# Routing between the output projection and the experts, rebuilt: all groups' choices at once, prefix counts by doubling sums, tile numbers by rounding, the one-hot in four parts

## The chip, the cores and the metric

One Trainium2 chip, one of its cores. The metric is the device time of one execution in microseconds; the executions of the kernel before are compared by their median. All data are float32.

## The reference, cut to what matters

One trunk layer on 256 context and 1,024 latent tokens (T = 1,280, D = 1,024): mixers, then a mixture of experts, then a last norm. The change touches only the choice of experts and the lists made from it:

```
gp = softmax(t @ w_rg + b_rg)              # 4 groups
g_top, g_idx = top_k(gp, 1)
el = (t @ w_re + b_re).reshape(T, 4, 4)    # 4 experts in each group
ep = softmax(el of the chosen group)
e_top, e_idx = top_k(ep, 2)
wts = e_top / sum(e_top) * g_top
y = sum over the two experts of wts * (silu(t @ w_gate) * (t @ w_up)) @ w_down
```

## The kernel before

Five instruction streams (PE, DVE, ACT, POOL, SP) are written out by hand, each in the order of the source, and meet on counting semaphores. Nothing is scheduled by a program. Every VectorE (DVE) operation of the routing waits for the one ahead of it (`dve_chain`); the ones that another engine waits for count `dve_once` up, and TensorE (PE) answers on `pe_once`.

Tokens stand in NT = 10 tiles of 128. After the output projection, each tile gets its normed rows `h2`, which SP stores to HBM (`h2_store`), while `x2_store` stores the residual. `router` (PE, L1278) multiplies the turned rows by the routers' 20 columns, and `logits` (DVE, L2089) puts them into `lg`: per tile 4 columns of groups and 4 x 4 of experts. Then the routing runs once for all tokens:

1. DVE chooses the group (`top`, five operations on 10 x 4), picks out its four logits with a one-hot (`r_big`, L2192), chooses the first and the second expert (`top` twice), and makes `m_one`, `m_two` and their sum `m_all`: 16 columns for each of 10 tiles, and an empty eleventh (L2203 to L2207). ACT computes the exponentials for the weights meanwhile (L1628), which DVE turns into `wts` (L2217 to L2225).
2. PE counts, for each token and expert, the tokens ahead of it: a product with a triangle (L1300) for those of its own tile, and ten products with ones (L1302), 160 to 16 columns wide, for those of earlier tiles.
3. DVE turns counts into the number of slot tiles of each expert (L2231 to L2250) and a slot for each of the 2 x 10 choices of a token (`r_pos`, L2256). A slot number is split in a tile (one of MT = 35, `r_hi`) and a lane (one of 128, `r_lo`): 36 thresholds are compared and summed (L2259, L2261), their differences are the one-hot `r_hot` (L2265). From it come `r_hot_w` (times the weight) and `r_hot` (times the token's number), and `r_lane` is the lane's one-hot, 20 x 128 (L2271).
4. PE adds up 20 products of `r_lane` with `r_hot` (L1307), which give the token of every slot, and 20 with `r_hot_w` (L1310), which give its weight. Meanwhile DVE makes the tables `tab_i` of expert addresses (L2275 to L2287), then, from the first product, the list `slot_i` (L2290).
5. POOL gathers the rows of a slot tile from HBM by `slot_i` (L2510), PE turns them (`turn_slots`, L1320), ACT copies them (L1636), and `gate_up` (L1325), `hidden` and `down` (L1335) follow, for 35 slot tiles. SP loads experts' weights into a ring of four: experts 0 to 2 during the routing, expert 3 only when the routing's scratch, over which it lies, is free. `landing_told` passes the arrival of an expert's weights on to PE.

Of the kernel before, what the change touches and what calls it, by code (L numbers as in the profile page):

```python
# [18 lines left out]
ALU = mybir.AluOpType  # L19
# [3 lines left out]
P = 128  # L23
# [4 lines left out]
NT = T // P  # L28
# [12 lines left out]
RING_E = len(RING_AT)  # L41
COL = dict(aq=0, ak=512, av=640, dq=768, dk=1280, dv=1792, ba=2304, dgate=2336, gattn=2848, gdn=3872)
# [32 lines left out]
def small_constants():  # L75
# [3 lines left out]
            [float(at[e + 1] - at[e]) if e + 1 < NE else 0.0 for e in range(NE)], 128.0 * np.arange(MT + 1), np.arange(P) - 128.0, [4, 3, 2, 1],  # L79
# [15 lines left out]
def build(nc, a, outs):  # L95
    ctx = ExitStack()
    with ctx:
# [47 lines left out]
        slot_step, k128, lane, first4, turn_of = small_row(NE), small_row(MT + 1), small_row(P), small_row(4), small_row(NE)  # L145
# [351 lines left out]
        r_gm, r_m1, r_m2, r_seen = [rsc(NT, 1) for _ in range(4)]  # L497
        r_ohg, r_oh1, r_oh2, r_key, r_el, r_el2 = [rsc(NT, 4) for _ in range(6)]
        r_e5 = rsc(NT, 5)
        r_big = rsc(NT * NE)  # L500
        m_both = rsc(2, NT * NE)
        m_all = rsc(NT + 1, NE)
# [4 lines left out]
        r_hi, r_lo, tok_f = rsc(2 * NT), rsc(2 * NT), rsc(2 * NT)  # L507
        r_ge, r_hot = rsc(2 * NT, MT + 1), rsc(2 * NT, MT)
        r_tab = rsc(HT + MT + NE)
        r_hot_w = flat(r_ge)[:, 0:2 * NT * MT].rearrange("p (j t) -> p j t", t=MT)  # L510
# [20 lines left out]
        def _(sp):  # L531
# [273 lines left out]
        def _(pe):  # L805
# [492 lines left out]
            router(OUT_LAST)  # L1298
            pe.wait_ge(S["dve_once"], 7)
            mm(ps[:, 4, 0:(NT + 1) * NE], before, flat(m_all), start=True, stop=False)  # L1300
            for n in range(NT):
                last = mm(ps[:, 4, (n + 1) * NE:(NT + 1) * NE].rearrange("p (n e) -> p n e", e=NE), ones,  # L1302
                          m_all[:, n, :].unsqueeze(1).to_broadcast([P, NT - n, NE]), start=False, stop=(n == NT - 1))
            last.then_inc(S["pe_once"], 1)
            pe.wait_ge(S["dve_once"], 8)
            for j in range(2 * NT):
                last = mm(ps[:, 5, 0:MT], r_lane[:, j, :], r_hot[:, j, :], start=(j == 0), stop=(j == 2 * NT - 1))  # L1307
# [352 lines left out]
        def _(dve):  # L1660
# [507 lines left out]
            for t in OUT_PAIRS[-1] + (OUT_LAST,):  # L2168
                logits(t)
# [378 lines left out]
```

## Time and profile before

| | |
|---|---|
| Median of 3 executions | 2233.24 us (2230.2 to 2241.52) |
| Profiled execution: its own time | 2229.11 us |
| Its span in the trace | 2227.2 us |
| Busy share: PE, DVE, ACT, POOL | 91%, 48%, 29%, 17% |
| Granted TensorE clock, mean | 0.954 |

The times below are microseconds from the span's start. PE's records come in pairs: one float32 product is two records, so 20 products are "x40". In the lists of busy time a stage in which an engine waits hardly shows; it is read from the order of time.

### The profile page before, as it was taken

To read this page: it belongs to the slowest core of one execution; us is meant where nothing else is said; L and a number is where in the kernel's file an instruction comes from. 1 tells how busy PE (TensorE), PEld (TensorE's weight loads), DVE (VectorE), ACT (ScalarE), POOL (GpSimd) and SP (SyncE) were. 2 spreads that over 40 slices of the span, in tenths; PEclk is the share of its full clock that TensorE was granted. 3 is DMA by queue.
4 is the path that set the end of the run, shared out by engine and by line. 5 is a ranking of instruction groups with operands and counts; after the bars stand their busy time and mean duration, and the time that the engine had idled before them with its cause. 6 is when DMAs were issued, how large, how long until landed. Compare 5 with 4: busy or idle time off the path is not lost.

```text
span 2227.2 us, 40085 instructions
## 1 busy us (share of the span) xinstructions
PE 2022.2 (91%) x16735; PEld 1291.7 (58%) x16735; DVE 1063.1 (48%) x1868; ACT 640.2 (29%) x1329; POOL 381.6 (17%) x431
## 2 busy tenths in 40 slices
PE   4998999999999868888799999999899699999992
PEld 3556567676455457777656666666445644444441
DVE  2256665663687556656464223222554423333334
ACT  5222666663445323442330100100111111111112
POOL 2000100000000135543103122111220012222210
PEclk8999999999999979999999999999999599999996
DMA  9523300001010044443303232232333767698646
GB/s 335 170 76 116 84 5 2 1 1 58 21 32 0 13 64 76 77 74 63 102 0 104 62 81 57 58 84 76 136 111 123 238 190 201 185 282 231 185 76 217
DMA packets 261329, 226.44 MB, mean 102 GB/s; under 512 B 106588, under 2 KB 223648, under 8 KB 260256
## 3 DMA queue, kind: packets, MB, share of 16 engines
q1 hardware_dynamic: 249856, 184.98, 29.0%
q0 software_dynamic: 11296, 38.91, 7.8%
q8 instruction: 135, 2.21, 0.4%
q14 instruction: 42, 0.34, 0.0%
HBM read 175.15 MB, written 48.55 MB: 100 GB/s over the span
## 4 chain that ended last, share of the span: by engine, by line
PE 46%; DVE 3%; DMA 1%; ACT 1%; issue 0%; SPq 0%; DVEq 0%; ACTq 0%; POOLq 0%; PEldq 0%
PE ps L1176 17%; PE ps L1325 11%; PE ps L1335 5%; PE ps L1223 4%; PE ps L1164 3%; PE ps L1320 1%; PE ps L1278 1%; PE ps L1217 1%; DVE R L2350 1%; PE ps L1154 0%; PE ps L1268 0%; DMA R<-in_w_out_dram 0%; DMA R<-attn_out_scratch 0%; PE ps L1307 0%; PE ps L1310 0%
## 5 line engine op out<-in xcount | busy, mean ns | idle before, releaser
L1176 PE MATMUL ps<-R 128*128 128x320 f32 x1280 | 353.2, 436 | 3.0 <-DVEq L2040 2.3
L1176 PEld LDWEIGHTS ps<-R 128*128 128x128 f32 x1280 | 243.3, 191 | 110.7 <-DVE R L2079 7.9
L899 PE MATMUL ps<-R 128*128 128x512 f32 (+1 forms) x816 | 298.9, 525 | 4.9 <-DVE R L1707 1.8
L1325 PE MATMUL ps<-R 128*128 x560 | 248.8, 598 | 3.2 <-ACT R L1636 2.3
L899 PEld LDWEIGHTS ps<-R 128*128 128x128 f32 x816 | 155.4, 192 | 143.4 <-issue 132.2
L1325 PEld LDWEIGHTS ps<-R 128*128 128x128 f32 x560 | 107.4, 192 | 138.2 <-issue 138.2
L1773 DVE TENSOR_SCALAR_CACHE_REDUCE R<-ps 128x512 f32<-128x512 f32 (+1 forms) x208 | 128.3, 666 | 56.7 <-PE ps L995 56.6
L1335 PE MATMUL ps<-R 128*128 x280 | 126.2, 594 | 1.6 <-DVE R L2333 1.6
L1014 PEld LDWEIGHTS ps<-cst,R 128*128 128x128 f32 x800 | 86.4, 142 | 57.6 <-issue 45.9
L2333 DVE COPY R<-ps 128x256 f32<-128x256 f32 x35 | 14.8, 424 | 216.4 <-PE ps L1350 216.4
L1487 ACT ACTIVATE R<-R 128x1536 f32<-128x1536 f32 (+1 forms) x80 | 108.6, 1358 | 12.5 <-DVE R L1782 12.4
L1014 PE MATMUL ps<-cst,R 128*128 128x128 f32 x800 | 105.1, 280 | 4.5 <-ACT R L1497 2.9
L995 PE MATMUL ps<-R 64*128 64x512 f32 (+1 forms) x416 | 106.6, 616 | 2.3 <-SPq L590 2.1
L1645 ACT ACTIVATE R<-ps 128x256 f32<-128x256 f32 x35 | 13.4, 384 | 323.0 <-PE ps L1325 323.0
L2397 POOL TENSOR_TENSOR R<-cst,R 128x512 f32<-128x512 f32 x20 | 20.4, 1040 | 491.0 <-DVE R L1805 491.0
L1067 PE MATMUL ps<-R 64*64 64x64 f32 x2464 | 86.7, 226 | 15.7 <-issue 9.9
L1028 PE MATMUL ps<-R 128*64 128x128 f32 x1600 | 96.5, 276 | 0.5 <-ACT R L1513 0.5
L1497 ACT ACTIVATE R<-ps 128x512 f32<-128x512 f32 (+1 forms) x144 | 75.4, 571 | 73.6 <-PE ps L1014 73.2
L1223 PE MATMUL ps<-R 128*128 128x512 f32 x200 | 92.9, 619 | 2.4 <-DVE R L2098 2.4
L1067 PEld LDWEIGHTS ps<-R 64*64 64x64 f32 x2464 | 81.4, 141 | 18.6 <-issue 15.2
L1028 PEld LDWEIGHTS ps<-R 128*64 128x64 f32 x1600 | 86.8, 137 | 7.4 <-ACT R L1497 5.7
L2510 POOL DMA_INDIRECT R<-h_scratch,slot_i x35 | 34.3, 981 | 281.4 <-PE ps L1320 179.4
(343 smaller groups left out, 2885.6 us busy)
## 6 DMA issues: line engine op xcount, KB each, us to landing
R<-in_w_mod_dram SPq DMA_DIRECT2D x12, 2048.0 KB, 9.0
R<-in_w_in_dram SPq DMA_DIRECT2D x46, 512.0 KB, 5.4
R<-in_w_gate_e_dram SPq DMA_DIRECT2D x16, 1024.0 KB, 7.5
R<-in_w_up_e_dram SPq DMA_DIRECT2D x16, 1024.0 KB, 11.0
R<-in_w_down_e_dram SPq DMA_DIRECT2D x16, 1024.0 KB, 8.0
R<-tu_scratch SPq DMA_DIRECT2D x40, 256.0 KB, 4.4
R<-in_x_sample_dram SPq DMA_DIRECT2D x16, 512.0 KB, 6.7
token_sums<-R SPq DMA_DIRECT2D x10, 512.0 KB, 5.6
```

Source lines behind the costliest of these rows:

```text
L899: last = mm(ps[:, u % 4, 0:w], w_sb[n % NW][:, k, :], hT[:, k, c0:c0 + w], start=(k == 0), stop=(k == KD - 1))
L995: last = mm(ps[:, 2 * (u % 2) + g, 0:w], qT[lo, h4, qt * P:(qt + 1) * P], kT[lo, c0 + j * 512:c0 + j * 512 + w], start=True, stop=True)
L1014: last = turn128(ps[:, 4 + v % 3, k * P:(k + 1) * P], s_sb[i % 2][g][:, j * 512 + k * P:j * 512 + (k + 1) * P], ident)
L1028: last = mm(ps[lo, 7, (i % 4) * P:(i % 4 + 1) * P], v_sb[:, v0 + j, lo], pT[i % 2][g][:, j, :], start=(j == 0), stop=(j == nk - 1))
L1067: last = mm(ps[lo, bank, a * C:(a + 1) * C], lhs(a)[lo], rhs(a)[lo], start=True, stop=True)
L1176: last = mm(ps[:, bank, 0:HALF], lhs[:, k, :], rhs[:, k, :], start=(k == 0), stop=(k == 3))
L1223: last = mm(ps[:, bank, :], lhs[:, k, :], rhs[k], start=(k == 0), stop=(k == 3))
L1325: last = mm(ps[:, 2 + t % 2, :], hsT[t % 2][:, k, :], R[:, bass.ds(at + (RB + k * 512), 512)], start=(k == 0), stop=(k == KD - 1))
L1335: last = mm(ps[:, 5 + u % 3, :], hidT[t % 2][:, k, :], R[:, bass.ds(at + (RB + 4096 + k * D + h * 512), 512)], start=(k == 0), stop=(k == 1))
L1487: f(s_sb[i % 2][g][:, 0:w], s_sb[i % 2][g][:, 0:w], ACT.Exp, bias=shift[i % 2][g], accum_out=sums[qt % 2][:, g, h4:h4 + 1]).then_inc(S["p_ ...
L1497: f(pT[i % 2][g][:, 4 * j:4 * j + w // P, :].rearrange("p n c -> p (n c)"), ps[:, 4 + v % 3, 0:w], ACT.Copy).then_inc(S["pt_act"], 1)
L1773: v.tensor_scalar(s_sb[i % 2][g][:, j * 512:j * 512 + w], ps[:, 2 * (u % 2) + g, 0:w], HD ** -0.5, None, ALU.mult, ALU.max, accum_out=tops ...
```

## The change

- The choices of all four groups are made along with that of the group: `top` works on the 50 rows of 4 in `lg` (5 for each tile), twice instead of three times, and the chosen group masks the result. `m_all` is made first and lies in a zeroed strip `m_led`.
- The sums over earlier tiles are made by DVE (`r_sum2`, `r_sum4`, `r_sum8`, each the one before added to itself moved by 1, 2, 4 tiles, and then 8), and PE needs one product with ones in place of ten. PE's product with the triangle starts as soon as `m_all` is there.
- The tile of a slot is its number times 1/128, rounded by adding 1.5 x 2^23; `r_hot` is one comparison with 35 constants. `r_tok` is a tile of its own.
- `r_lane` is made in four parts of 2, 6, 6 and 6 choices, and PE starts on each as it comes.
- The weights (`r_e5`, ACT's exponentials, `wts`, `r_hot_w`) are made behind the one-hot; the last of them stand behind the tables and ahead of `slot_i`. `r_hot_w` lies in the residual's tile, so it waits until SP's stores of it have landed (`sp_out`).
- Of the 20 products that give the weights of the slots, 10 stand ahead of the first `turn_slots`, 10 ahead of the second `gate_up`; their result is copied in the second round.
- SP tells of the landing of experts 0 and 1 first, and loads expert 3 after the first two gathers have landed.
- The zeroing of `m_led` and three small operations stand ahead of the last logits.

The diff, with the repeated waits on `dve_chain` and the tile names' bookkeeping left out:

```diff
+ROUND = 1.5 * 2 ** 23
...
+        m_led = R3[:, 8960:8960 + (3 * NT + 11) * NE].rearrange("p (n e) -> p n e", e=NE)
+        m_pad, r_sum2, r_sum4 = m_led[:, 0:NT + 3], m_led[:, NT + 3:2 * NT + 6], m_led[:, 2 * NT + 6:]
+        m_all, r_sum8 = m_pad[:, 2:NT + 3, :], rsc(NT + 1, NE)
...
+        r_tok = R3[:, 8192:8192 + 2 * NT * MT].rearrange("p (j t) -> p j t", t=MT)
+        r_hot_w = R0[:, 0:2 * NT * MT].rearrange("p (j t) -> p j t", t=MT)
+        LANE_PARTS = ((0, 2), (2, 8), (8, 14), (14, 20))
...
             expert_load(2)
-            sp.wait_ge(S["dve_once"], 9)
-            sp.wait_ge(S["pe_once"], 5)
+            landing_told(0)
+            landing_told(1)
+            sp.wait_ge(S["dve_once"], 13)
             for n in (NT - 2, NT - 1):
                 sp.wait_ge(S[f"h2_out{n % 2}"], landed(n, 2))
+            for t in range(2):
+                sp.wait_ge(S[f"hs_in{t}"], 16)
             expert_load(3)
-            landing_told(0)
-            landing_told(1)
...
+            pe.wait_ge(S["dve_once"], 6)
+            mm(ps[:, 4, 0:(NT + 1) * NE], before, flat(m_all), start=True, stop=False)
             pe.wait_ge(S["dve_once"], 7)
...
+            mm(ps[:, 4, 0:(NT + 1) * NE], ones, flat(r_sum8), start=False, stop=True).then_inc(S["pe_once"], 1)
+            for part, (first, end) in enumerate(LANE_PARTS):
+                pe.wait_ge(S["dve_once"], 8 + part)
+                for j in range(first, end):
+                    last = mm(ps[:, 5, 0:MT], r_lane[:, j, :], r_tok[:, j, :], start=(j == 0), stop=(j == 2 * NT - 1))
             last.then_inc(S["pe_once"], 1)
...
+            def slot_weights(first, end):
+                for j in range(first, end):
+                    last = mm(ps[:, 7, 0:MT], r_lane[:, j, :], r_hot_w[:, j, :], start=(j == 0), stop=(j == 2 * NT - 1))
+                return last
+
+            pe.wait_ge(S["dve_once"], 13)
+            slot_weights(0, NT)
...
+                    if t == 1:
+                        slot_weights(NT, 2 * NT).then_inc(S["pe_once"], 1)
...
-            act.wait_ge(S["dve_once"], 6)
+            act.wait_ge(S["dve_once"], 12)
...
+            top(lgs, r_m1, r_oh1)
+            v.scalar_tensor_tensor(r_el2, r_oh1, -3e38, lgs, ALU.mult, ALU.add).then_inc(S["dve_chain"], 1)
...
             top(r_el2, r_m2, r_oh2)
...
+            v.tensor_tensor(r_key, r_oh1, r_oh2, ALU.add).then_inc(S["dve_chain"], 1)
...
+            v.tensor_tensor(by_group(m_all[:, 0:NT, :]), by_row(r_key)[:, :, 1:5, :], in_group, ALU.mult).then_inc(S["dve_once"], 1)
...
+            v.tensor_tensor(r_sum8[:, 8:NT + 1, :], r_sum8[:, 8:NT + 1, :], r_sum8[:, 0:NT - 7, :], ALU.add).then_inc(S["dve_once"], 1)
...
+            v.tensor_scalar(r_hm, pos, 1.0 / SLOTS, ROUND, ALU.mult, ALU.add).then_inc(S["dve_chain"], 1)
...
+            for first, end in LANE_PARTS:
+                v.tensor_tensor(r_lane[:, first:end, :], bc(r_lo[:, first:end].unsqueeze(2), [end - first, P]), bc(lane.unsqueeze(1), [end - first, P]), ALU.is_equal).then_inc(S["dve_once"], 1)
+                dve.wait_ge(S["dve_once"], count("dve_once"))
...
+            dve.wait_ge(S["sp_out"], 288 + 16 * NT)
+            v.tensor_tensor(r_hot_w, r_hot, bc(flat(wts).unsqueeze(2), [2 * NT, MT]), ALU.mult).then_inc(S["dve_chain"], 1)
...
             dve.wait_ge(S["pe_once"], 4)
             v.tensor_scalar(slot_i[:], ps[:, 5, 0:MT], -1.0, 0.0, ALU.add, ALU.max).then_inc(S["dve_once"], 1)
```

Line numbers of the kernel after are 8 to 27 higher. The order of DVE's instructions from the slots' numbers to the one-hot of the lanes, before (thresholds, their sum, lane, differences, weights, tokens, lanes, first table) and after (rounding, one-hot, tokens, tile, lane, lanes in two rows, weights' exponents, first table):

```order
L2259 TENSOR_TENSOR R<-R,small 128x720
L2261 TENSOR_REDUCE R<-R 128x20
L2263 SCALAR_TENSOR_TENSOR R<-R 128x20
L2265 TENSOR_TENSOR R<-R 128x700
L2267 TENSOR_TENSOR R<-R,wts 128x700
L2269 TENSOR_TENSOR R<-R 128x700
L2271 TENSOR_TENSOR R<-R,small 128x2560
L2275 TENSOR_TENSOR R<-small,R 128x560
```

```order
L2264 TENSOR_SCALAR R<-R 128x20
L2266 TENSOR_TENSOR R<-R,small 128x700
L2268 TENSOR_TENSOR R<-R 128x700
L2270 TENSOR_SCALAR R<-R 128x20
L2272 SCALAR_TENSOR_TENSOR R<-R 128x20
L2275 TENSOR_TENSOR R<-R,small 128x256
L2275 TENSOR_TENSOR R<-R,small 128x768 x3
L2278 TENSOR_TENSOR R<-R 128x10x4
L2280 TENSOR_TENSOR R<-R 128x50
L2282 TENSOR_TENSOR R<-R 128x40
L2284 TENSOR_REDUCE R<-R 128x10
L2288 TENSOR_TENSOR R<-small,R 128x560
```

Two operations as long as the tables' are gone, the long one is four, and four small ones stand between it and the tables. The order of DVE's instructions from the tables' end to `slot_i`, which before are L2285 to L2290 and after L2298 to L2317:

```order
L2283 TENSOR_REDUCE R<-R 128x35
L2285 TENSOR_SCALAR R<-R 128x16
L2287 CAST tab_i<-R 128x86
L2290 TENSOR_SCALAR slot_i<-ps 128x35
L2302 TENSOR_SCALAR mod_row<-ps 128x35
```

```order
L2298 TENSOR_SCALAR R<-R 128x16
L2300 CAST tab_i<-R 128x86
L2303 TENSOR_REDUCE R<-R 128x10
L2305 TENSOR_SCALAR R<-R 128x10
L2307 TENSOR_TENSOR R<-R 128x10
L2309 RECIPROCAL wts<-R 128x10
L2311 TENSOR_TENSOR wts<-wts,R 128x10
L2314 TENSOR_TENSOR R<-R,wts 128x700
L2317 TENSOR_SCALAR slot_i<-ps 128x35
```

Six operations of the weights have moved in ahead of `slot_i`. The order of PE's products from the end of the counting to the first turn of gathered rows, before and after (one row is a product here, not two records):

```order
L1302 MATMUL ps<-R,cst 128x32
L1302 MATMUL ps<-R,cst 128x16
L1307 MATMUL ps<-R 128x35 x20
L1310 MATMUL ps<-R 128x35 x20
L1320 MATMUL ps<-cst,R 128x128 x8
```

```order
L1308 MATMUL ps<-R,cst 128x176
L1310 MATMUL ps<-R,cst 128x176
L1314 MATMUL ps<-R 128x35 x20
L1319 MATMUL ps<-R 128x35 x10
L1331 MATMUL ps<-cst,R 128x128 x8
```

Ten of the weights' products have gone from the place ahead of the first turn; they stand behind the second turn now.

## Rows read from the trace of the kernel before

**Rows 1.** The chain that ended last, 1690 to 1830: start us, us, what
```profile
1762.80 8.75 PE ps L1307 x40
1771.55 8.55 PE ps L1310 x40
...
1781.19 1.14 SPq L755
...
1782.81 9.67 PE ps L1325 x16
...
1795.60 7.13 PE ps L1325 x16
...
1802.94 0.87 PE ps L1320 x8
```
**Rows 2.** Windows: us, PE, PEld, DVE, ACT, POOL busy (instructions), PEclk, DMA share, GB/s
```profile
1730.00:1760.00 30.00, 12.41 (x54) 11.67 (x54) 18.42 (x57) 2.72 (x4) 0.00 (x0) 0.50 1.06 362
...
1760.00:1765.00 5.00, 2.20 (x11) 2.20 (x11) 4.86 (x5) 0.00 (x0) 0.00 (x0) 0.50 0.40 156
...
1785.00:1790.00 5.00, 5.00 (x9) 1.98 (x9) 0.00 (x0) 0.00 (x0) 0.00 (x0) 0.71 1.05 365
```
**Rows 3.** Timeline of DVE, choices and weights: start us, busy us, line, op, tiles, shapes
```profile
1739.18 0.20 DVE L2172 TENSOR_REDUCE R<-R 128x10 f32<-128x40 f32 x1
1739.41 0.20 DVE L2174 TENSOR_TENSOR R<-R 128x40 f32<-128x40 f32 x1
...
1740.58 0.43 DVE L2192 TENSOR_TENSOR R<-R 128x160 f32<-128x160 f32 x1
...
1744.17 0.69 DVE L2203 TENSOR_TENSOR R<-R 128x160 f32<-128x160 f32 x2
...
1746.00 0.19 DVE L2217 TENSOR_REDUCE R<-R 128x10 f32<-128x40 f32 x1
...
1746.89 0.18 DVE L2225 TENSOR_TENSOR wts<-wts,R 128x10 f32<-128x10 f32 x1
```
**Rows 4.** Timeline of DVE, from the counts to the list of slots
```profile
1750.71 0.33 DVE L2231 TENSOR_TENSOR R<-ps,small 128x160 f32<-128x160 f32 x1 [3.64 <-PE ps L1302]
...
1755.05 0.91 DVE L2259 TENSOR_TENSOR R<-R,small 128x720 f32<-128x720 f32 x1
1756.00 0.90 DVE L2261 TENSOR_REDUCE R<-R 128x20 f32<-128x720 f32 x1
...
1762.78 0.74 DVE L2275 TENSOR_TENSOR R<-small,R 128x560 f32<-128x560 f32 x1
...
1766.30 0.21 DVE L2287 CAST tab_i<-R 128x86 int32<-128x86 f32 x1
1771.66 0.20 DVE L2290 TENSOR_SCALAR slot_i<-ps 128x35 uint32<-128x35 f32 x1 [5.15 <-PE ps L1307]
```
**Rows 5.** Timeline of PE around the routing
```profile
1705.77 3.65 PE L1278 MATMUL ps<-R 128*128 128x20 f32 x32
...
1735.26 3.60 PE L1278 MATMUL ps<-R 128*128 128x20 f32 x16 [0.73 <-ACT R L1605]
1745.41 0.95 PE L1300 MATMUL ps<-R,cst 128*128 128x176 f32 x2 [6.55 <-DVE R L2207]
...
1779.89 1.95 PE L1320 MATMUL ps<-cst,R 128*128 128x128 f32 x8
```
**Rows 6.** Timeline of POOL, the first gather's issue
```profile
1772.14 1.07 POOL L2510 DMA_INDIRECT R<-h_scratch,slot_i  x1 [101.68 <-DVE slot_i L2290]
```
**Rows 7.** DMA issues: first gather; residual's last store (issued 1734.67): us to landing
```profile
R<-h_scratch,slot_i POOLq DMA_INDIRECT x1, 4.4
...
token_sums<-R SPq DMA_DIRECT2D x1, 512.0 KB, 9.9
```
**Rows 8.** All 35 gathers, line L2510
```profile
DMA to landing us min/median/max: 4.2/4.8/8.5
```
**Rows 9.** Timeline of ACT, the table for the exponentials
```profile
1744.21 1.28 ACT L1628 ACT_TABLE_LOAD   x1 [9.00 <-DVE R L2200]
```

More of the change, by code:

```diff
@@ L78, in small_constants @@
     rows = [np.arange(T // SLOTS) * float(SLOTS), np.arange(HT), (np.arange(NE)[None, :] < np.arange(NE)[:, None]).ravel(),
-            [float(at[e + 1] - at[e]) if e + 1 < NE else 0.0 for e in range(NE)], 128.0 * np.arange(MT + 1), np.arange(P) - 128.0, [4, 3, 2, 1],
+            [float(at[e + 1] - at[e]) if e + 1 < NE else 0.0 for e in range(NE)], ROUND + np.arange(MT), np.arange(P) - 63.5, [4, 3, 2, 1],
             [int(f"{e:04b}"[::-1], 2) for e in range(NE)]]
@@ L1298, in _ @@
             router(OUT_LAST)
+            pe.wait_ge(S["dve_once"], 6)
+            mm(ps[:, 4, 0:(NT + 1) * NE], before, flat(m_all), start=True, stop=False)
             pe.wait_ge(S["dve_once"], 7)
[L1300 to L1303, printed above, removed]
-            last.then_inc(S["pe_once"], 1)
-            pe.wait_ge(S["dve_once"], 8)
-            for j in range(2 * NT):
-                last = mm(ps[:, 5, 0:MT], r_lane[:, j, :], r_hot[:, j, :], start=(j == 0), stop=(j == 2 * NT - 1))
-            last.then_inc(S["pe_once"], 1)
-            for j in range(2 * NT):
-                last = mm(ps[:, 4, 256:256 + MT], r_lane[:, j, :], r_hot_w[:, j, :], start=(j == 0), stop=(j == 2 * NT - 1))
-            last.then_inc(S["pe_once"], 1)
-            pe.wait_ge(S["dve_once"], 9)
+            mm(ps[:, 4, 0:(NT + 1) * NE], ones, flat(r_sum8), start=False, stop=True).then_inc(S["pe_once"], 1)
[3 more added lines that the diff above has]
+                    last = mm(ps[:, 5, 0:MT], r_lane[:, j, :], r_tok[:, j, :], start=(j == 0), stop=(j == 2 * NT - 1))
+            last.then_inc(S["pe_once"], 1)
+            def slot_weights(first, end):
[4 more added lines that the diff above has]
+            slot_weights(0, NT)
             def turn_slots(t):
@@ L2226, in _ @@
             dve.wait_ge(S["dve_chain"], count("dve_chain"))
+            v.tensor_tensor(r_sum8[:, 8:NT + 1, :], r_sum8[:, 8:NT + 1, :], r_sum8[:, 0:NT - 7, :], ALU.add).then_inc(S["dve_once"], 1)
+            dve.wait_ge(S["dve_once"], count("dve_once"))
+            for i, oh in enumerate((r_oh1, r_oh2)):
+                v.tensor_tensor(by_group(m_both[:, i, :].rearrange("p (n e) -> p n e", n=NT)), by_row(oh)[:, :, 1:5, :], in_group, ALU.mult).then_inc(S["dve_chain"], 1)
+                dve.wait_ge(S["dve_chain"], count("dve_chain"))
@@ L2272, in _ @@
+            v.tensor_reduce(r_e5[:, :, 4:5], r_gap, AX.X, ALU.add).then_inc(S["dve_once"], 1)
             dve.wait_ge(S["dve_once"], count("dve_once"))
```

126 lines of the change are left out of this document (62 added, 64 removed).

## The prediction

> **What bounds the kernel now.** I read the chain of work that ended last first. Among the experts it is TensorE (PE) alone, one slot tile behind the other, and nothing of that is changed. Ahead of it stands one long passage in which PE is mostly without work or at small work, and that is the change's place: from the first routing operation at 1739.18 [rows 3] to the first `gate_up` at 1782.81 [rows 1], 43.6 us. Whatever moves that start moves the end by as much, unless the first slot tiles give it back.
>
> The passage has five pieces, and the reader should see who is waited for in each. (a) 1739.18 to 1745.41: VectorE (DVE) chooses, and PE's count starts at 1745.41 [rows 3, 5]. (b) To 1750.71: DVE needs PE's counts, and its row says that it sat 3.64 us for L1302 [rows 4]. (c) To 1762.80: DVE alone, up to the one-hot of the lanes [rows 1, 4]. (d) 1762.80 to 1780.10 (1771.55 + 8.55): 40 products of 35 columns, 8.75 and 8.55 us [rows 1]. The first half ends at 1771.55 and `slot_i` follows at 1771.66 [rows 1, 4]; the gather is issued at 1772.14 and has landed 4.4 us later, at 1776.5 [rows 6, 7]. So the second half, 1771.55 to 1780.10, covers the gather and 3.6 us more. (e) Turns from 1779.89, and `gate_up` at 1782.81, released by SP's L755, the issue of expert 3's weights, which stands ahead of `landing_told(0)` [rows 1, 5].
>
> From 1730 on all of it runs at the granted clock 0.50, 1.2 GHz, and the clock comes back to 1.00 inside 1785 to 1790: the share 0.71 says 2.9 us of five at half, thus at about 1787.9, 5.1 us after `gate_up` began [rows 2].
>
> **A price for DVE.** From one start to the next an operation on 40 elements takes 0.23 us (1739.18 to 1739.41) and one on 720 takes 0.95 (1755.05 to 1756.00) [rows 3, 4]. The line through both is 0.19 us + 1.06 ns for each element: 160 cost 0.36, 176 0.37, 200 0.40, 256 0.46, 700 0.93, 768 1.00. Two rows bound it: two operations of 160 took 0.69 together, one with a stride 0.43 [rows 3]. The changed code reads with strides in a few places, so about 0.1 each is open.
>
> **The change, part by part.**
> *Choices.* Ahead of `m_all` stand 12 operations on 200 and one on 160: 4.80 + 0.36 = 5.16 us, so PE can begin at 1744.4 in place of 1745.41. The group's own choice is no longer a step of its own, but each step is five times as wide: a gain of only 1.0.
> *Prefix sums.* Three additions on 176 and one on 48: 3 x 0.37 + 0.24 = 1.36, done at 1745.7. The triangle's product (0.95 for a product of 176 [rows 5]) is behind them by then. The ones' product takes 0.95 more, to 1746.7, and DVE starts at 1746.8 where it started at 1750.71: 3.9 gained so far. The two masks for `m_both`, 0.7 us, lie beside PE's product.
> *To the one-hot.* The code up to `r_pos` is unchanged: 1750.71 to 1755.05, 4.34 us [rows 4], now ending at 1751.15. Then two of 700 and three of 20 elements: 1.86 + 0.63 = 2.49, to 1753.65, and the first part, 256 elements, to 1754.1. PE starts at 1754.15, not 1762.80: 8.65 gained. In place of seven operations stand six shorter ones, and PE no longer waits for the whole one-hot.
> *The products.* 40 records take 8.75, so one product takes 0.44. Two are done at 1755.0, the second part is there at 1755.1, each later part takes DVE 1.00 and PE 2.6, so PE runs on: 1755.15 + 18 x 0.44 = 1763.05. DVE could start on `slot_i` at 1763.15.
> *DVE's list ahead of `slot_i`.* Parts to 1757.1; four small operations, 0.94, to 1758.05; tables 1762.78 to 1766.54 before [rows 4], 3.76, to 1761.8; five for the weights, 1746.00 to 1747.10 [rows 3], 1.10; `r_hot_w` 0.93. Sum 1763.85: this, 0.7 later than PE's result, is what `slot_i` waits for. ACT has from 1758.05 to 1761.8 for a table load of 1.28 [rows 9] and the exponentials; hidden, by 2 us.
> *Gather.* Issued 0.48 behind the start of `slot_i`, 1764.3; landed 4.4 later, 1768.7. PE's ten products for weights run from 1764.1 to 1768.5: the cover and the gather end within 0.2 us, the gather last. Turns start at 1768.8 instead of 1779.89: 11.1 gained. With the cover cut in half it no longer costs anything, and the gather is what is late now.
> *To `gate_up`.* From the turns' start to `gate_up` it was 2.9 us. The wait for SP's issue is gone, since the landings are told first, but the turns end 1.95 after their start [rows 5] and ACT's last copy must still follow, so at most 1.0 can fall away, and likely little. I take 2.9 again: start at 1771.7, **11.1 us earlier**.
> *The other ten weights' products.* From the end of the first `gate_up` (1782.81 + 9.67 = 1792.48) to the second it is 3.12 us, in which PE turns (0.87) and then sits for ACT's sigmoid, with its table load, and copies [rows 1]. The ten products go there: 20 records at the full clock by 32 records in 3.65 us, 0.114 each [rows 5], are 2.28, and 0.87 + 2.28 = 3.15. They cost nothing within 0.1 as long as the clock is full; at half, by 16 records in 3.60 [rows 5], they are 4.5 and cost 2.2.
> *What else moves, at nothing.* Zeroing 656 elements (under 0.95, by the operation on 720 [rows 4]) and three small operations stand ahead of the last logits. These wait for PE's last router, 1735.26 to 1738.86 [rows 5], just ahead of the first choice at 1739.18; the zeroing lies beside it or before. Without that cover it costs 1.5. Expert 3 is loaded after two gathers, about 1771, not 1781, and its first tile is far off. The copy of the weights' result is 0.2 on DVE, which has spare time beside PE in each slot tile.
>
> *A rule against the row.* The first gather landed 4.4 us after issue [rows 7]. The Trainium skill, page "DMA: Bandwidth & Descriptors", section "Anatomy of one DMA", gives for a transfer issued from GpSimd 2.0 us and its bytes over 436 GB/s; for 512 KB that is 3.2. By that figure, an estimate from the page, the products for weights would end last, and the gain would be 11.3. The sum above keeps to the row.
>
> **Sum.** 1.0 from the choices, 2.9 from the counts, 4.75 from the shorter way to the one-hot and its parts, minus 0.8 because `slot_i` now waits for DVE and not for PE's product, plus 3.3 since half the weights' products have left the passage (the gather's landing decides now). 11.15, less what rounding takes: **11.1**. The profiled execution took 2229.11 (span 2227.2), so it would be 2218.0; the median of the three is 2233.24, 4.1 above that execution, and from it I get **2222**. That is 0.50%, exactly the bound of about 0.5% that a measurement of this kernel can tell from no change. The sign is fairly sure and the class isn't.
>
> **The rivals.**
> *The clock comes back at another moment.* `gate_up` took 9.67 with 5.1 us at half, 7.13 at full [rows 1, 2]: 2.5 us were lost. If it comes back almost at once, gain up to 13.6, time 2219.6; if the whole first `gate_up` stays at half (14.3), and the ten products with it, gain 11.1 - 4.6 - 2.2 = 4.3, 2229; a half step of that, 8.5, 2225. For earlier: nothing but the spread. For later: the passage before it is shorter and has two more pauses. Earlier 15%, later 11%.
> *The gather is slow.* It is issued nearly 8 us earlier, closer to the loads of experts 0 to 2. The slowest of 35 took 8.5 us [rows 8]. Then gain 11.1 - 4.1 = 7.0, 2226. Against: traffic ended at about 1762 (a share of 0.40 in 1760 to 1765 [rows 2]), 2 us before the issue. 8%.
> *Cutting the one-hot costs a pause.* If a cut of a long DVE operation brought a pause about as long as a part, 1.0, instead of the 0.19 that the line gives, three cuts move the tables and `slot_i` by 2.4: gain 8.7, 2224.5. Against: the operation of 720 took 0.91 and the next began 0.04 later [rows 4]. 2%. The Trainium skill, page "VectorE: DVE Perf Modes", section "The DRAIN you can't avoid", has such a pause, the operation's duration less 266 ns, behind each operation; the trace doesn't agree.
> *Slower: `slot_i` is held by the residual's store.* `r_hot_w` waits for all stores of the residual, and `slot_i` stands behind it. The last store took 9.9 us among 9 MB of weights and landed at 1744.6 [rows 7]; DVE asks at 1762.9. Each us beyond costs one: at 1774.0 nothing is gained, and past 1785 it is slower by over 0.5%; a landing at 1790 gives 2249. Against: 18 us of room. 4%, with whatever else is on that side.
>
> **How the numbers follow.** The forecast (gain 9.5 to 12.8, thus 2220.4 to 2223.7) has 60%; a share of 35 lies above 0.5%, 25 below, as the centre is on the bound. Faster: 35 + 15 (early clock) = 0.50. Same: 25 + 11 + 8 + 2 = 0.46. Slower: 0.04. The range goes from the early clock less what three executions scatter (2219.6 - 3 = 2216) to a late clock or a slow gather with it (2226 + 4 = 2230). If the strided operations cost 0.1 more each and DVE's line is off by 5%, that is 1 us, inside it.
>
> **What would show it.** In the trace after: PE's counting product within 0.3 of 1744.4; DVE's first use of the counts at 1746.8; the first slot product at 1754.1 and the last ending by 1763.1; `slot_i` idle for nothing, right behind L2314, at 1763.85; the turns released by the gather; `gate_up` at 1771.7; 3.1 us from the end of the first to the second. Wrong if PE waits between the parts, if the turns start later than 1770, or if the second `gate_up` comes over 4 us behind the first.

## The result, and the profile after

Over eight timed runs of each kernel the changed one took 2219.36 us (2215.72 to 2223.43) and the one before 2231.76 (2230.2 to 2241.52): 12.4 us less. The ratio over all runs is 0.9941, with a 95% interval of 0.9926 to 0.9955: the changed kernel is faster by 0.45 to 0.74%. That is clear of no change, takes in the bound of 0.5% that the prediction named, and by a line of 2% would count as the same. The forecast was 2222 and a gain of 11.1. The profiled execution took 2222.26, its span 2220.4.

That span is only 6.8 us shorter than before's, and this is no contradiction. The first routing choice came at 1739.18 [rows 3] before and comes at 1745.38 now. In the executions of the changed kernel's repeat and of its variants below it came between 1737.3 and 1748.9, though all of them are the same up to the last router's product. So all times below are taken from the first choice, a row that each kernel has (`DVE L2172` before, the first `DVE L2193` now), up to the first `gate_up`. This stretch is called the passage.

Timeline of PE in the changed kernel (start us, busy us, line, operation, tiles, and in brackets the idle time ahead with what ended it), the answer to [rows 1, 5]:
```profile
1750.56 0.95 PE L1308 MATMUL ps<-R,cst 128*128 128x176 f32 x2 [5.50 <-DVE R L2219]
1751.93 0.96 PE L1310 MATMUL ps<-R,cst 128*128 128x176 f32 x2 [0.42 <-DVE R L2227]
1760.30 8.89 PE L1314 MATMUL ps<-R 128*128 128x35 f32 x40 [7.42 <-DVE R L2275]
1770.46 4.48 PE L1319 MATMUL ps<-R 128*128 128x35 f32 x20 [1.27 <-DVE slot_i L2317]
1775.03 1.97 PE L1331 MATMUL ps<-cst,R 128*128 128x128 f32 x8
1777.94 8.94 PE L1336 MATMUL ps<-R 128*128 x16 [0.94 <-ACT R L1649]
1786.72 1.04 PE L1331 MATMUL ps<-cst,R 128*128 128x128 f32 x8
1787.59 2.32 PE L1319 MATMUL ps<-R 128*128 128x35 f32 x20
1789.90 7.13 PE L1336 MATMUL ps<-R 128*128 x16
```
Timeline of DVE, the answer to [rows 3, 4]:
```profile
1745.17 0.18 DVE L2102 TENSOR_TENSOR R<-ps,b_r 128x20 f32<-128x20 f32 x1 [4.63 <-PE ps L1286]
1745.38 0.36 DVE L2193 TENSOR_REDUCE R<-R 128x50 f32<-128x200 f32 x1
...
1752.99 0.33 DVE L2236 TENSOR_TENSOR R<-ps,small 128x160 f32<-128x160 f32 x1 [0.40 <-PE ps L1310]
...
1759.82 3.40 DVE L2275 TENSOR_TENSOR R<-R,small 128x256 f32<-128x256 f32 x4
...
1769.28 0.89 DVE L2314 TENSOR_TENSOR R<-R,wts 128x700 f32<-128x700 f32 x1 [0.26 <-DVE wts L2311]
1770.21 0.19 DVE L2317 TENSOR_SCALAR slot_i<-ps 128x35 uint32<-128x35 f32 x1
```
The chain that ended last, where it leaves DVE:
```profile
1769.28 0.90 DVE R L2314
1770.68 4.30 DMA R<-h_scratch,slot_i
1775.03 1.98 PE ps L1331 x8
1777.10 0.61 ACT R L1649
1777.94 8.94 PE ps L1336 x16
```
And the windows (us, busy of PE, PEld, DVE, ACT, POOL, then the granted clock, DMA share, GB/s), the answer to [rows 2]:
```profile
1744.00:1759.00 15.00, 2.97 (x9) 1.95 (x9) 12.27 (x36) 0.00 (x0) 0.00 (x0) 0.50 1.06 381
1759.00:1776.00 17.00, 14.34 (x65) 14.00 (x66) 11.20 (x29) 1.53 (x2) 2.02 (x2) 0.50 0.77 260
1776.00:1781.00 5.00, 4.06 (x9) 2.11 (x8) 0.00 (x0) 1.19 (x2) 0.93 (x1) 0.50 0.45 144
1781.00:1786.00 5.00, 5.00 (x12) 2.09 (x11) 0.00 (x0) 0.00 (x0) 0.00 (x0) 0.94 0.99 356
```
DVE's first row shows that the zeroing and the small operations that now stand ahead of the last logits cost nothing, as the prediction had it: DVE still waits 4.63 for PE's last router there. DVE's wait for the counts is 0.40 where it was 3.64. PE begins the slot products with the first of four parts (`x4` in one row). The chain no longer has the second forty products in it: it goes from DVE over the gather to the turns.

In us behind the first choice:

| | before | predicted | after |
|---|---|---|---|
| PE's triangle product | 6.23 | 5.2 | 5.18 |
| DVE's first use of the counts | 11.53 | 7.6 | 7.61 |
| first slot product | 23.62 | 15.0 | 14.92 |
| `slot_i` | 32.48 | 24.67 | 24.83 |
| first gather landed | 37.3 | 29.5 | 29.6 |
| first turn | 40.71 | 29.6 | 29.65 |
| first `gate_up` | 43.63 | 32.5 | 32.56 |
| first `gate_up`, duration | 9.67 | 9.67 | 8.94 |
| its end to the second | 3.12 | 3.15 | 3.02 |

The passage is 11.07 shorter. From the first choice to the end it is 488.06 before and 475.02 after, 13.0 less: 11.07 of the passage, 0.72 of the first `gate_up`, 0.1 of the gap behind it, and 1.15 from the second `gate_up` to the end. At most 11.9 of that, up to the second `gate_up`, can be the change's. From the second to the 35th `gate_up` it takes 376.15 to 376.17 in all 14 profiled executions of this document, and from the 35th to the end 55.49 before, 54.33 after and 53.99 to 55.71 over the changed kernel and its variants: the 1.15 lies in that last stretch and within its scatter.

### The profile page after: what moved, and what is told of

It is laid out like the page before. It is cut to its first block, busy times and chain, and to the rows that moved or that the text cites. A ratio compares the mean times of both kernels' runs of the same rounds, so it can differ in the third digit from the quotient of the medians.

```text
span 2220.4 us, 40051 instructions
## 1 busy us (share of the span) xinstructions
PE 2014.9 (91%) x16717; PEld 1283.5 (58%) x16717; DVE 1065.7 (48%) x1871; ACT 640.2 (29%) x1329; POOL 381.1 (17%) x431
## 4 chain that ended last, share of the span: by engine, by line
PE 54%; DVE 5%; issue 3%; DMA 2%; ACT 1%; PEld 0%; SPq 0%; POOL 0%; DVEq 0%; ACTq 0%; POOLq 0%; PEldq 0%
PE ps L1184 17%; PE ps L1336 11%; PE ps L1346 5%; PE ps L1231 4%; PE ps L1075 3%; PE ps L1172 3%; PE ps L1081 3%; PE ps L1331 1%; PE ps L1225 1%; PE ps L1286 1%; PE ps L893 1%; DVE R L2377 1%; PE ps L883 1%; PE ps L1162 0%; PE ps L885 0%
## 5 line engine op out<-in xcount | busy, mean ns | idle before, releaser
L1500 ACT ACTIVATE R<-R 128x1536 f32<-128x1536 f32 (+1 forms) x80 | 108.6, 1358 | 12.5 <-DVE R L1795 12.4
L2075 DVE TENSOR_TENSOR R<-ps,R 128x320 f32<-128x320 f32 x16 | 7.9, 492 | 154.1 <-PE ps L1184 154.1
```

The source lines that it names most:

```text
L1500: f(s_sb[i % 2][g][:, 0:w], s_sb[i % 2][g][:, 0:w], ACT.Exp, bias=shift[i % 2][g], accum_out=sums[qt % 2][:, g, h4:h4 + 1]).then_inc(S["p_ ...
```

## The experiments

Each kernel is the changed one with the edit shown. A passage of 32.56 is what is to be compared with; each passage is read from one profiled execution. The times stand with their ratio to the kernel before and its 95% interval, except for two kernels that were run once. Every one of these intervals overlaps the changed kernel's own (0.9926 to 0.9955), so the times alone tell none of these kernels from it, and what an edit costs is read from the traces. The edits were made one at a time, and what they cost are not parts that add up to 11.07.

**cover_whole**: all twenty weights' products ahead of the first turn.
```diff
-            slot_weights(0, NT)
+            slot_weights(0, 2 * NT).then_inc(S["pe_once"], 1)
...
-                    if t == 1:
-                        slot_weights(NT, 2 * NT).then_inc(S["pe_once"], 1)
```


> The changed kernel, but all 20 of the weights' products stand ahead of the first turn again. My theory, that the gather's landing decides once only ten products cover it: PE runs 40 records at half clock, 8.75 us, behind slot_i instead of 4.4, and the first gather has landed long before, so the turns start at slot_i + 9.0, 4.2 us later against slot_i than in the changed kernel (where it was 4.8), and the passage from the first choice to the first gate_up is 36.8 us, not 32.6. The gap between the first two gate_ups stays at 3.0 to 3.1. Gain over the kernel before about 8. Rival, that the earlier slot_i alone makes the gain and the products were hidden anyway: passage 32.6, gain over the kernel before unchanged at 12.

Passage 36.52, with `slot_i` at 24.83 and the gather landed at 29.72 as in the changed kernel. Its timeline of PE:
```profile
1762.33 8.75 PE L1319 MATMUL ps<-R 128*128 128x35 f32 x40 [1.27 <-DVE slot_i L2315]
1770.89 1.95 PE L1331 MATMUL ps<-cst,R 128*128 128x128 f32 x8
```
The turns start at 33.63 with the gather long there, so the second half is worth 3.96 us. The time is 2222.38 (ratio 0.9971, 0.9952 to 0.999). The rival fell.

**onehot_whole**: the one-hot in one part (the counts that other engines wait for move with it).
```diff
-        LANE_PARTS = ((0, 2), (2, 8), (8, 14), (14, 20))
+        LANE_PARTS = ((0, 20),)
```


> The changed kernel, but the lanes' one-hot is made by one operation of 2560 elements. My theory, by the sum: PE's 20 slot products start when the whole is there, 2.86 us behind the operation's start (0.48 with parts), and run 8.75 without a pause; DVE's list is 0.6 shorter, but slot_i now waits for PE and not for DVE, about 11.7 us behind the one-hot's start where it was 10.4: 1.3 us later, passage 33.9. Rival A, the parts are worth nothing since DVE's list decides anyway: slot_i 0.6 earlier, passage 32.0. Rival B, the whole earlier start of PE counts: 2.4 later, passage 35.0.

Passage 34.04: the first product at 17.31 and `slot_i` at 26.17, now held by PE. Time 2220.91 (0.9964, 0.9949 to 0.9978).
```profile
1764.93 0.89 DVE L2314 TENSOR_TENSOR R<-R,wts 128x700 f32<-128x700 f32 x1
1768.00 0.19 DVE L2317 TENSOR_SCALAR slot_i<-ps 128x35 uint32<-128x35 f32 x1 [2.18 <-PE ps L1314]
```
The parts give 1.5, though the first product comes 2.4 earlier by them: the rest is eaten by DVE, which becomes the later of the two. What else brought the first product forward, the rounding in place of the thresholds and the weights' move behind the one-hot, was not taken back by itself; it is read from the rows of DVE alone.

**ten_products**: ones' products by tile in place of the doubling sums.
```diff
-            mm(ps[:, 4, 0:(NT + 1) * NE], ones, flat(r_sum8), start=False, stop=True).then_inc(S["pe_once"], 1)
+            for n in range(NT):
+                last = mm(ps[:, 4, (n + 1) * NE:(NT + 1) * NE].rearrange("p (n e) -> p n e", e=NE), ones,
+                          m_all[:, n, :].unsqueeze(1).to_broadcast([P, NT - n, NE]), start=False, stop=(n == NT - 1))
+            last.then_inc(S["pe_once"], 1)
```


> The changed kernel, but PE sums over the earlier tiles with ten products with ones, as before, and DVE's doubling sums are left out. My theory: from the start of PE's triangle product to DVE's first use of the counts it takes 5.3 us as before, not 2.4 us, so everything behind is 2.9 us later: passage 35.5, gain over the kernel before about 9. Rival, DVE's four sums cost what PE's products cost: passage 32.6 unchanged.

Passage 35.33, counts at 10.47, `slot_i` at 27.46. Time 2219.72 (0.9959, 0.9941 to 0.9977). Its timeline of PE:
```profile
1743.37 0.95 PE L1308 MATMUL ps<-R,cst 128*128 128x176 f32 x2 [5.49 <-DVE R L2221]
1744.11 4.45 PE L1310 MATMUL ps<-R,cst 128*128 128x160 f32 x20
```
4.45 us of PE against four additions and one product: 2.8 us, and all of it arrives at `gate_up`.

**told_late**: expert 3's weights issued ahead of `landing_told(0)` and `(1)`, as before.
```diff
-            landing_told(0)
-            landing_told(1)
...
+            landing_told(0)
+            landing_told(1)
```


> The changed kernel, but SP tells PE of the landing of experts 0 and 1 behind the issue of expert 3's load again. My theory: that issue now waits for both first gathers and takes about 2.3 us, so the first gate_up waits for SP and not for ACT's copy, starting about 2.6 us behind the second gather's landing: 2.2 us later than in the changed kernel, passage 34.8. Rival, the order of the two is worth at most the 0.3 us that it was in the kernel before: passage 32.9.

Passage 34.57: 2.0 more. Time 2221.33 (0.9958, 0.9938 to 0.9979). Its timeline of PE, and then the chain:
```profile
1777.07 9.34 PE L1336 MATMUL ps<-R 128*128 x16 [2.78 <-SPq L771]
```
```profile
1774.54 0.37 SPq L757
...
1774.95 0.58 SPq L757
...
1775.58 1.29 SPq L762
...
1776.92 0.02 SPq L771
```
With the shorter passage SP's issues would have stood in the way; the second gather's landing, which SP awaits ahead of them, comes too late for them to be hidden. In the prediction's sum the moved lines gained nothing, yet without them the change would have given 2 us less.

**after_again**: the changed kernel, unchanged, to learn what belongs to it and what to the execution.

> The changed kernel once more, unchanged, beside the kernel before, to see what of a difference in the whole time comes from the change's place. My theory: passage from the first choice to the first gate_up 32.6 us in this profile too (within 0.3), the rest of the span apart from the clock's return at the first gate_up the same, and what lies ahead of the first choice scatters by several us from one execution to the next; gain over the kernel before 11 to 13 us. Rival, the change shifts something ahead of itself (its first choice came 6.2 us later in the first profile): then the first choice is again at 1745, not between 1737 and 1743 as in the four kernels derived from it.

Passage 32.52, first choice at 1742.43, first `gate_up` 8.82, from the choice to the end 474.51. Time 2218.46 (0.9944, 0.9924 to 0.9964). The passage repeats within 0.04; what lies ahead of it doesn't.

**all_in_gap**: all twenty weights' products behind the second turn, none beside the gather.
```diff
-            pe.wait_ge(S["dve_once"], 13)
-            slot_weights(0, NT)
...
-                        slot_weights(NT, 2 * NT).then_inc(S["pe_once"], 1)
+                        slot_weights(0, 2 * NT).then_inc(S["pe_once"], 1)
```


> The changed kernel, but none of the weights' 20 products stands ahead of the first turn; all stand ahead of the second gate_up. My theory, that the gather's landing and not the ten products decides the turns' start, and that the gap between the first two gate_ups holds ten products and no more: passage 32.6 as in the changed kernel, within 0.1, and from the end of the first gate_up to the start of the second 5.4 us (0.87 for the turns, 40 records of 0.114), where it was 3.0: 2.4 us slower than the changed kernel. Rival A, the ten products still held the turns back: passage up to 0.2 shorter. Rival B, the gap has room: 3.0 to 3.5.

Passage 32.49, and 5.10 to the second `gate_up`. Time 2221.57 (0.9966, 0.9946 to 0.9986). Its timeline of PE:
```profile
1769.39 1.97 PE L1329 MATMUL ps<-cst,R 128*128 128x128 f32 x8 [5.80 <-DMA R<-h_scratch,slot_i]
1772.31 9.89 PE L1334 MATMUL ps<-R 128*128 x16 [0.94 <-ACT R L1647]
...
1782.91 4.55 PE L1319 MATMUL ps<-R 128*128 128x35 f32 x40
```
Ten products less beside the gather change nothing: the gather alone decides, and it lands no sooner beside an idle PE (29.53). In the gap ten are free and twenty cost 2.1. All forty records there ran at the full clock, and it stayed up behind them: the granted clock is 1.00 in every window from 1778 to 1840.

**slot_first**: `slot_i` ahead of `r_hot_w`, and eight weights' products in place of ten ahead of the turn.
```diff
-            dve.wait_ge(S["sp_out"], 288 + 16 * NT)
-            v.tensor_tensor(r_hot_w, r_hot, ...).then_inc(S["dve_chain"], 1)
             v.tensor_scalar(slot_i[:], ps[:, 5, 0:MT], -1.0, 0.0, ALU.add, ALU.max).then_inc(S["dve_once"], 1)
+            dve.wait_ge(S["sp_out"], 288 + 16 * NT)
+            v.tensor_tensor(r_hot_w, r_hot, ...).then_inc(S["dve_once"], 1)
```


> The changed kernel, but slot_i is made ahead of r_hot_w, and of the first ten of the weights' products eight stand ahead of the first turn and two behind it. My theory, by the sum (slot_i waited for DVE's list and not for PE): slot_i at 23.9 us behind the first choice, not 24.8, the first gather lands at 28.7, eight products end at 28.6, the turns start at 28.75 and the first gate_up at 31.7, 0.9 us earlier than in the changed kernel; the two products fit in the 0.94 us in which PE waits for ACT's copy. Rival A, PE's slot products set slot_i: no change, 32.6. Rival B, the products now end behind the landing, or the two do not fit: between 32.0 and 32.6.

A miss: passage 32.60. `slot_i` came at 24.25, 0.58 earlier and not 0.9, since it now waited 0.62 for PE's products; but the gather landed at 29.64, as if nothing had been moved. Time 2218.32 (0.9947, 0.9927 to 0.9967). Timeline of POOL in it, and then of DVE:
```profile
1768.24 1.58 POOL L2538 DMA_INDIRECT R<-h_scratch,slot_i  x1 [90.05 <-DVE slot_i L2315]
```
```profile
1767.76 0.20 DVE L2315 TENSOR_SCALAR slot_i<-ps 128x35 uint32<-128x35 f32 x1 [0.62 <-PE ps L1314]
1767.99 0.89 DVE L2318 TENSOR_TENSOR R<-R,wts 128x700 f32<-128x700 f32 x1
```
POOL's issue took 1.58 instead of 1.07, the first packet left 2.29 after its start and not 1.78, and landing took 4.91, not 4.30. It began 0.25 us into DVE's operation on 700. From the first packet to landing it took 2.62, and 2.52 in the changed kernel: nearly all of the delay lies in the issue.

**small_beside**: the test of that cause. The four small operations for `put_i` directly behind `slot_i`, then `r_hot_w`; six products ahead of the turn, two behind it, twelve in the gap (`slot_weights(0, 6)`, `(6, 8)` and `(8, 20)`).

> As slot_first, but the four small operations of the put list stand between slot_i and r_hot_w, so that only they lie beside POOL's issue of the gather; six of the weights' products stand ahead of the first turn, two behind it, twelve in the gap. In slot_first POOL's issue took 1.58 us and not 1.07, the first packet came 2.29 us behind the issue's start and not 1.78, and the landing 4.9 and not 4.3 behind it. Theory, that r_hot_w (700 columns on VectorE) beside the issue did this: issue 1.07, first packet 1.8, landing 4.3, the first gather landed 29.05 behind the first choice, first gate_up at 32.0, and the gap 0.45 longer. Rival, that the tail of the experts' loads did it (their last packet ended 0.6 us before slot_first's gather was issued, 1.0 in the changed kernel): issue and landing as in slot_first.

POOL's issue is 1.07 again, the first packet 1.78, landing 4.36 and the passage 32.05, which is 0.5 shorter. The rival fell: the loads' last packet ended 0.44 ahead of the issue, closer than slot_first's 0.56. By the second `gate_up` the half us is spent: it starts at 44.39, and at 44.52 and 44.36 in the two executions of the changed kernel, since twelve products in the gap make it longer. One run, 2219.27. Timeline of POOL:
```profile
1767.31 1.07 POOL L2538 DMA_INDIRECT R<-h_scratch,slot_i  x1 [93.45 <-DVE slot_i L2315]
```

**warm**: thirteen products of 512 columns added on PE (four, seven and two), whose result nobody reads, to have the clock up early.
```diff
+            def filler(n):
+                for _ in range(n):
+                    mm(ps[:, 3, :], ident, cst[:, 0:512], start=True, stop=True)
```


> The changed kernel with added products of 512 columns that nobody reads: 4 behind the last router, 7 behind the counting products, 2 behind the first ten weights' products. They lie in time in which PE waits. It measures what the half clock costs in this passage. Theory: the clock is back at 1.00 before the slot products, these are then paced by DVE's parts, but slot_i stays at 24.8 (DVE's list); the weights' products take 2.3 and not 4.4 (nothing, the gather decides), the turns 1.0 and not 2.0, so gate_up starts at 31.7, and it takes 7.1 and not 8.9; the second gate_up starts 41.8 behind the first choice, 2.7 us earlier than in the changed kernel's profile, and the scatter of the first gate_up is gone. Rival A, the added products come in the way (7 of them at half clock take 8.4 us, where 7.4 are free): slot products a us or more late, gate_up at 33 or more. Rival B, the clock falls again among the small products: gate_up takes 8.6 to 9.7 as now.

A miss: `gate_up` at 34.84, the second one at 44.99 (44.52 in the changed kernel). Time 2219.24 (0.9945, 0.9927 to 0.9964). Its windows:
```profile
1748.00:1758.00 10.00, 8.47 (x24) 3.82 (x23) 9.11 (x27) 0.00 (x0) 0.00 (x0) 0.98 1.05 369
1758.00:1763.00 5.00, 4.64 (x24) 4.53 (x23) 4.69 (x10) 1.51 (x2) 0.00 (x0) 0.57 1.10 351
1763.00:1776.00 13.00, 11.60 (x44) 9.29 (x44) 4.87 (x16) 0.01 (x1) 2.03 (x2) 0.51 0.47 169
```
The clock came up to 2.4 GHz during the added products and was back at 1.2 GHz at about 1758.7, 1.2 us after the slot products of 35 columns had begun; ahead of them PE had been idle for 1.42. Rival B, the clock falling again, holds for the slot products, but `gate_up` took 7.13. What failed in the theory is the price of the last two added products: they ran at half, 3.76 us, ended about 3 us behind the gather's landing (29.49) and held the turns up. The expectation had 8.4 us for seven of them at half; an estimate from this row is 13.

**dense_expert2_early**: `slot_i` directly behind the products, tables and weights after it, and added products also between the parts of the slot products (4, 8, 1, 1 and 2, unread).

> The changed kernel with slot_i made as soon as PE has it (the weights' operations and the tables behind it), and added products of 512 columns that nobody reads: 4 behind the last router, 8 behind the counting products, 1 each behind the first and second part of the slot products, 2 behind the last. Expert 2 is loaded where it was. Theory, if the clock stays at 1.00 through the slot products: they end 21.3 us behind the first choice and not 23.8, slot_i at 21.4, but the gather, issued at 21.9, meets the loads of experts 0 to 2, whose last packet is at 24.3, and lands only at about 28 (6 us and more, where it was 4.3). First gate_up at about 30, taking 7.1; the second 40, against 44.5. Rival A, the clock falls in between as in the run with fewer added products: slot products at half clock, 10 to 12 us for them with the added ones, slot_i at 26 or later, slower than the changed kernel in the passage. Rival B, the gather is not slowed: landed at 26.2.

Timeline of PE in it, and then a window:
```profile
1747.29 7.03 PE L1312 MATMUL ps<-cst 128*128 128x512 f32 x16
1754.87 0.63 PE L1323 MATMUL ps<-R 128*128 128x35 f32 x4 [0.56 <-DVE R L2287]
1755.34 1.10 PE L1312 MATMUL ps<-cst 128*128 128x512 f32 x2
1756.28 1.42 PE L1323 MATMUL ps<-R 128*128 128x35 f32 x12
...
1758.48 2.76 PE L1323 MATMUL ps<-R 128*128 128x35 f32 x24
...
1767.10 1.97 PE L1342 MATMUL ps<-cst,R 128*128 128x128 f32 x8 [1.00 <-DMA R<-h_scratch,slot_i]
1770.01 8.57 PE L1347 MATMUL ps<-R 128*128 x16 [0.94 <-ACT R L1661]
```
```profile
1747.00:1766.00 19.00, 17.81 (x86) 11.35 (x86) 15.11 (x39) 1.53 (x2) 2.32 (x2) 1.00 1.02 346
```
With wide products in between, the clock stayed at 2.4 GHz through the slot products, 40 records in 6.4 us with all the added ones; `slot_i` came at 21.02, the gather landed at 26.71 and `gate_up` started at 29.67, the second at 41.26: 3.3 us earlier than in the changed kernel. The choice to the end is 471.72. The clock still fell ahead of the turns: `gate_up` took 8.57 and not 7.1, and so the second came 1.3 later than expected. The time, 2216.04 (0.9941, 0.9923 to 0.996), doesn't stand out from the changed kernel's 0.9941 and 0.9944.

**dense_expert2_late**: the same with expert 2's weights issued behind the two gathers, since the gather now comes close to the loads.

> As dense_expert2_early, but expert 2 is loaded behind the first gathers, with expert 3. Theory, that the traffic slows an earlier gather: it lands 4.3 us behind its issue and not 6 or more; first gate_up at 28.3 where the clock stays up, about 2 us earlier than with the load where it was; expert 2 itself is not waited for. Rival: no difference between the two within 0.5.

The gather took 5.39, not less than the 5.22 above, though the loads' last packet ended 6.6 us ahead of its issue: the loads are not what makes it slower than 4.3. The theory fell and the rival, no difference within 0.5, held. `gate_up` at 29.17, choice to end 473.12, time 2217.76 (0.9939, 0.992 to 0.9958). So by time neither of the two is a version that clearly beats the changed kernel; only their traces are shorter.

**tables_behind_gather**: the early one, with VectorE's tables held until the gather has landed.
```diff
+            dve.wait_ge(S["hs_in0"], 16)
             ends = r_cmp[:, 0:HT * NE].rearrange("p (t e) -> p t e", t=HT)
```


> Open is why the first gather of the two kernels with products added in the passage lands 5.2 to 5.4 us after its issue and not 4.3. In both of them VectorE's seven operations for the tables (two of 560 elements wide, two reductions over 560) lie beside the gather's packets; in the changed kernel VectorE has nothing but small operations then. This kernel is the early one of the two with one wait more: the tables start when the first gather has landed. Theory, VectorE's wide operations hold the gather up: it lands 4.2 to 4.5 us after its issue, 25.9 behind the first choice. Rival, it is something else (PE's clock or products, the earlier moment): 5.1 to 5.4. The tables then end 3.8 us behind the landing and PE's registers wait for them, so the first gate_up starts at about 30.3 by the theory and 31.2 by the rival, later than 29.67 in both; the time itself says nothing at this size.

Landed 4.72 after the issue, between the two expectations, and the passage 31.83 with the tables in the way, 0.6 longer than even the rival's 31.2. One run, 2222.79. Timelines of POOL and of DVE in it:
```profile
1767.23 1.07 POOL L2550 DMA_INDIRECT R<-h_scratch,slot_i  x1 [90.21 <-DVE slot_i L2300]
1768.60 1.25 POOL L2550 DMA_INDIRECT R<-h_scratch,slot_i  x1 [0.30 <-issue]
1774.23 1.13 POOL L2550 DMA_INDIRECT R<-h_scratch,slot_i  x1 [4.38 <-PE ps L1342]
```
```profile
1768.13 0.89 DVE L2314 TENSOR_TENSOR R<-R,wts 128x700 f32<-128x700 f32 x1
1772.04 0.74 DVE L2318 TENSOR_TENSOR R<-small,R 128x560 f32<-128x560 f32 x1 [3.02 <-DMA R<-h_scratch,slot_i]
...
1773.80 0.74 DVE L2324 TENSOR_TENSOR R<-R,small 128x560 f32<-128x560 f32 x1
```
The wide table operations account for about 0.5 of the 0.9. The cause of the remaining 0.4 is open. `r_hot_w` stayed beside the second issue (1.25 instead of 0.96), but in small_beside too it ran ahead of the gather's first packets, and there landing took 4.36. The gather is also issued earlier than in the changed kernel, and the load of expert 2 is still under way, with its last packet 3.0 us after the issue. None of these was tried alone, and each of these landings is read from one execution.

The issues of this run and of the others also show how a wide operation of DVE holds an issue up. What counts is how long the one that is running when the issue starts still has to run: 0.64 us in slot_first lengthened the issue by 0.51, 0.42 (the second issue here and in both dense runs) by 0.28 to 0.29, 0.31 (the third here, beside `L2324`) by 0.19, and 0.25 (the second in small_beside) by 0.11, each against the same issue in the changed kernel. Each time it is that rest less about 0.13. A wide operation that started only 0.45 into the issue (the first of the tables, in the dense runs) added nothing: 1.24 with it, 1.25 without.

## Why the prediction was right

*The counts and the choices.* "A gain of only 1.0": 1.05. "3.9 gained so far": 11.53 - 7.61 = 3.92. ten_products puts 2.8 of it on the doubling sums, where the sum had 2.9. DVE's price line held: from the start of an operation on 700 to the next it took 0.92 to 0.93, where 0.93 was predicted.

*The one-hot.* First product predicted 14.97 from the first choice, measured 14.92. The products took 8.89 in all, and 8.90 was predicted (1754.15 to 1763.05): PE waited once, 0.12 for the second part, about the 0.1 that the working had, and never after that. Its list of signs of being wrong names any wait between the parts, so that sign was drawn tighter than its own working.

*`slot_i` waits for DVE.* Right: it stands directly behind `L2314`. It was to start at 24.67 and started at 24.83; DVE paused 0.26 ahead of `r_hot_w`, which the list didn't have. onehot_whole shows the other side: there PE is the later one, by 2.18.

*The gather decides.* Landed 4.30 after its issue where 4.4 was taken from the row. The chain names it, and all_in_gap shows that PE's ten products beside it cost nothing. The estimate from the Trainium skill, page "DMA: Bandwidth & Descriptors", section "Anatomy of one DMA", was 3.2 for it; no first gather of these runs took under 4.2, so the row was the right one. For the weights' products the sum had 3.3. From `slot_i` to the first turn it was 8.23 before and is 4.82 now, 3.41 less, which is the term as the sum has it. cover_whole measures 3.96 for the split by itself: the term came from before's cover, which overhung the gather by 3.6, while in the changed kernel's order a whole cover overhangs it by 3.9 (33.63 against 29.72).

*To the first `gate_up`.* "I take 2.9 again": 2.91. It rests on the new order of the landings: by told_late it would have been 4.8. The prediction named the wait that fell away but not that it would otherwise have grown by 2: leaving the order as it was would have cost the change 2 us that no term of its sum shows.

*The first `gate_up` and the gap.* The gap is 3.02 where 3.15 was predicted. `gate_up` took 8.94 and not 9.67, as in the early-clock case but by less than a third of it. This can't be put down to the change: over the nine executions of the changed kernel and its variants whose passage ran at half clock the first `gate_up` took 8.65 to 9.89, and 8.82 in the changed kernel's repeat. Why the clock comes back earlier in one than in another was not looked into.

*The rivals.* The residual's last store landed 5.8 us behind the first choice and was asked for 18 us later: the slower side was never near. No pause came with the cut: four parts of the one-hot follow each other in 3.40 us. The slow gather didn't come. The forecast of 60% is met by the gain (12.4, within 9.5 to 12.8) but not by the time (2219.36, where it had 2220.4 to 2223.7). The time also lies next to that of the early clock, 2219.6, and that is chance: the traces show under a third of that case.

*The size.* Up to the first slot product the sum had 8.65 (1.0, 2.9 and 4.75) and 8.70 was measured; for the handover from PE to DVE minus 0.8, measured minus 1.05; for the weights' products 3.3, measured 3.41. 11.1 was foreseen and 11.07 stands in the trace. Each step held and the two misses, of 0.25 and 0.1, have opposite signs, so that the agreement within 0.03 is partly luck. The medians differ by 12.4: 0.83 more than the passage is the first `gate_up` and the gap, and the rest lies within what executions scatter. The predicted 2222 was higher than 2219.36 for one more reason: it was counted from a median of three, 2233.24, where eight give 2231.76. The prediction gave 0.50 to faster and 0.46 to the same, with the bound at 0.5%; the interval takes in that bound, so the result doesn't settle it.

## What to carry to other kernels

Cost a serial passage engine by engine, and ask at each handover who is late *after* the edit. Here two cuts of PE's work ended on other limits, DVE's list and the gather, so that one of 2.4 us gave 1.5 and one cover could shrink for nothing. When a passage gets shorter, look at what was hidden in it: SP's issues cost next to nothing before and would have cost 2.0 afterwards. When the spread of whole runs is as large as the edit, measure from an instruction that both kernels have; it repeated within 0.04 us in the two traces of the changed kernel, where whole runs of one kernel spread over 2.7 to 18.4.

## What the runs showed of the hardware

- A wide VectorE operation that was running when GpSimd's issue of an indirect transfer began held the issue up: 1.58 instead of 1.07 us, first packet 2.29 instead of 1.78, with one f32 operation on 700 elements from two inputs in SBUF. So moving the list of slots 0.58 earlier gained nothing until its neighbour was changed. Over six issues in five runs the delay was what the operation still had to run, less about 0.13 us (0.64 left gave 0.51, 0.25 left gave 0.11). Small operations (10 to 35 elements) didn't do it, nor did a wide one on 560 that started 0.45 us into the issue. All the wide ones that did had two inputs in SBUF and none of the small ones running at an issue's start had, so the runs don't tell width from the number of inputs.
- TensorE's clock beside products of 35 columns: in warm it had stood at 2.4 GHz for some 10 us and fell to 1.2 GHz 1.2 us after they began (0.98, then 0.57 and 0.51 granted), and in the changed kernel the 17 us that hold them ran at 0.50. With products of 512 columns in between it stayed at 1.00 from 1747 to 1766. That the narrow products themselves bring it down is not shown: in warm an idle time of 1.42 stood ahead of them, 0.56 in the run with the wide ones, and in all_in_gap forty such records, 4.4 us behind a `gate_up` and its turns, ran at 1.00 without a fall. At half a record of 35 columns takes 0.22 us, at full 0.115.
- The first gather landed 4.25 to 4.56 us after its issue in the ten executions without a wide VectorE operation at the start of its issue or beside its packets, 4.9 where its issue was held up, and 5.2 and 5.4 where VectorE ran wide operations beside its packets. With those taken away it took 4.7, of which 0.4 is not explained.
